# A gated delta rule scan: heads in halves, two products of the state beside each other, the decay on ScalarE, the last token tile finished by itself

## The reference, cut to what matters

```python
def step(state, inp):
    qd, wc, uc, kd, aqk, dl = inp
    v_new = uc - jnp.einsum('bhik,bhkv->bhiv', wc, state)
    o = jnp.einsum('bhik,bhkv->bhiv', qd, state) + jnp.einsum('bhij,bhjv->bhiv', aqk, v_new)
    state = state * dl[..., None, None] + jnp.einsum('bhik,bhiv->bhkv', kd, v_new)
    return state, o
...
state0 = jnp.zeros((bn, h, dk, dv), jnp.float32)
_, o = lax.scan(step, state0, xs)
...
y = (o * lax.rsqrt(jnp.mean(o * o, axis=-1, keepdims=True) + RMS_EPS)
     * norm_gain.astype(jnp.float32) * jax.nn.silu(zf))
```

## Time and profile before

| | us |
|---|---|
| median of three runs | 1775.05 |
| the profiled execution: its time | 1778.09 |
| the profiled execution: its span on the core | 1776.8 |

### The profile page before, as it was taken

How to read it: one execution, slowest core, us unless ns; L and a number is a source line. 1 busy time by engine, 2 the same in 40 slices (tenths; PEclk the granted TensorE clock), 3 DMA queues, 4 the chain that set the end, 5 groups by cost and what they waited for, 6 DMA issues and landing times.

```text
span 1776.8 us, 25041 instructions
## 1 busy us (share of the span) xinstructions
PE 1625.4 (91%) x9620; PEld 1177.3 (66%) x9620; DVE 922.4 (52%) x1873; ACT 694.2 (39%) x1518; POOL 347.1 (20%) x353
## 2 busy tenths in 40 slices
PE   6999869789999999989997799999999959999992
PEld 5887559667888888867877466667888733333330
DVE  4752665455766665664526866643435752223224
ACT  4432752353333334454322677764424421111111
POOL 0000643001222210000000455530010122333320
PEclk9999989899999999989998799999999969999997
DMA  6321000321444443323200000015223349999964
GB/s 273 115 95 48 1 2 3 143 95 58 188 181 190 189 178 154 131 95 141 97 0 25 1 8 8 8 36 232 95 93 145 142 166 383 394 370 392 385 249 159
DMA packets 40229, 251.74 MB, mean 142 GB/s; under 512 B 17904, under 2 KB 18032, under 8 KB 23600
## 3 DMA queue, kind: packets, MB, share of 16 engines
q1 hardware_dynamic: 23120, 223.49, 32.2%
q10 hardware_dynamic: 3168, 15.07, 2.2%
q0 software_dynamic: 13824, 11.58, 2.0%
HBM read 293.99 MB, written 18.87 MB: 176 GB/s over the span
## 4 chain that ended last, share of the span: by engine, by line
PE 85%; DVE 7%; DMA 3%; ACT 3%; issue 1%; SPq 0%; POOL 0%; DVEq 0%; ACTq 0%; POOLq 0%
PE banks L2222 17%; PE banks L2224 16%; PE banks L2223 16%; PE banks L2690 8%; PE banks L2160 7%; PE banks L2706 4%; PE banks L2283 3%; PE banks L2305 3%; DMA plain<-in_moe_gu,arena 2%; PE banks L2407 1%; PE banks L2569 1%; DVE units L1210 1%; ACT arena L629 1%; PE banks L2612 1%; PE banks L2539 0%
## 5 line engine op out<-in xcount | busy, mean ns | idle before, releaser
L629 ACT ACTIVATE units<-arena 128x512 fp32r<-128x512 f32 (+2 forms) x416 | 251.0, 626 | 482.1 <-PE banks L2224 477.3
L1210 DVE TENSOR_TENSOR units<-arena,units 128x512 fp32r<-128x512 f32 x370 | 252.2, 705 | 281.1 <-ACT units L629 280.8
L2222 PE MATMUL banks<-hx,units 128*128 128x512 f32 x800 | 316.3, 395 | 3.5 <-DVE arena L1663 1.7
L2224 PE MATMUL banks<-hx,units 128*128 128x512 f32 x800 | 313.3, 392 | 0.0
L2223 PE MATMUL banks<-hx,units 128*128 128x512 f32 x800 | 313.3, 392 | 0.0
L2222 PEld LDWEIGHTS banks<-hx,units 128*128 128x128 f32 x800 | 151.7, 190 | 35.5 <-issue 4.5
L2224 PEld LDWEIGHTS banks<-hx,units 128*128 128x128 f32 x800 | 151.4, 189 | 31.9
L2223 PEld LDWEIGHTS banks<-hx,units 128*128 128x128 f32 x800 | 151.7, 190 | 31.0
L2160 PE MATMUL banks<-arena 128*128 128x128 f32 (+2 forms) x752 | 118.1, 292 | 49.6 <-ACT arena L629 14.1
L629 ACT ACTIVATE arena<-banks 128x512 f32<-128x512 f32 (+3 forms) x194 | 106.7, 563 | 143.8 <-PE banks L2160 65.9
L2222 PE MATMUL banks<-units 128*128 128x512 f32 x380 | 150.8, 397 | 8.7 <-DVE units L1210 8.7
(11 more groups left out here) (420 smaller groups left out, 2448.6 us busy)
## 6 DMA issues: line engine op xcount, KB each, us to landing
arena<-in_moe_gu SPq DMA_DIRECT2D x32, 2048.0 KB, 10.0
arena<-in_w_in SPq DMA_DIRECT2D x17, 2048.0 KB, 8.6
arena<-in_moe_dn SPq DMA_DIRECT2D x32, 1024.0 KB, 9.8
arena<-in_ada SPq DMA_DIRECT2D x12, 2048.0 KB, 11.0
arena<-in_w_gu SPq DMA_DIRECT2D x11, 2048.0 KB, 8.5
arena<-in_w_out SPq DMA_DIRECT2D x4, 2048.0 KB, 8.5
arena<-in_w_down SPq DMA_DIRECT2D x4, 2048.0 KB, 10.6
arena<-in_cmp_w SPq DMA_DIRECT2D x2, 2048.0 KB, 8.5
```

The lines of the kernel that those rows point to most:

```text
L629: return func(dst, src, ACT.Copy, scale=scale)
L1210: tt(lo, src, hi.bitcast(F32), SUB).then_inc(*up("gemm_dve", "lo", c.part, u))
L2222: pe.matmul(bs[i], sh[:, q], mh, start=c.first and k == 0, stop=False)
L2224: return pe.matmul(bs[i], sl[:, q], mh, start=False, stop=c.last and k == c.kn - 1)
```

## The change

- TensorE gives `ws` and `dS` two banks each, one for each half of the heads (0 and 1, 2 and 3), and the waits on S and `vn` go by halves. VectorE's additions for `vn` and S go by halves as well, 256 columns each.
- `o` is written to the other 64 partitions (`other`), and head by head `ws` and the first `o` product are issued in turn.
- In chunk 0 the state is zero: `ws`, the first `o` product and the clearing of S are left out, `vn` is U itself, and the next state is a copy of `dS`.
- The decay `Sd` moves from VectorE to ScalarE, as four copies of 128x128 with a factor per partition.
- A small square root ahead of the scan brings in the function table; the means' roots are taken in two parts (`goA` for tiles 0 to 2, `goB` for tile 3).
- Tiles 0 to 2 are scaled and transposed first; tile 3 is scaled by VectorE in four instructions that include the gate z (GpSimd's fourth product goes), and its transposes go to two banks of their own (`yL`).
- The load of `gu0` now waits for that work of VectorE on tile 3.

```diff
@@ -940,19 +940,29 @@
     for t in range(4):
         a.wait_ge(*at("gdn_pe", "U", t))
         copy(m.U[:, t, :], s.bank("gdn", "U", t)).then_inc(*up("gdn_act", "U", t))
+    func(m.rs_tmp[:, 63:64], ones1, ACT.Sqrt)
     for c in range(8):
-        t, rows = c // 2, H64[c % 2]
+        t, rows, other = c // 2, H64[c % 2], H64[1 - c % 2]
+        if 0 < c < 7:
+            for h, q in enumerate(H4):
+                a.wait_ge(*at("gdn_dve", "S", c, h // 2))
+                copy(m.Sd[:, q], m.S[c % 2][:, q], m.dl[:, c, h:h + 1]).then_inc(*up("gdn_act", "Sd", c, h // 2))
+        if c == 7:
+            root("goA", g[:, 1, 0:12], m.rs_tmp[:, 0:12])
         a.wait_ge(*at("gdn_pe", "o", c))
-        copy(m.O[rows, t, :], s.bank("gdn", "o", c)[rows, :]).then_inc(*up("gdn_act", "O", c))
+        copy(m.O[rows, t, :], s.bank("gdn", "o", c)[other, :]).then_inc(*up("gdn_act", "O", c))
         if c % 2:
             a.wait_ge(*at("gdn_act", "O", c))
             for h in range(4):
                 func(m.osq[:, t, H4[h]], m.O[:, t, H4[h]], ACT.Square,
                      accum_out=g[:, 1, 4 * t + h:4 * t + h + 1]).then_inc(*up("gdn_act", "osq", t, h))
-    root("go", g[:, 1, :], m.rs_tmp[:, 0:16])
-    for f in (0, 2):
+    root("goB", g[:, 1, 12:16], m.rs_tmp[:, 0:4])
+    for f in range(4):
         a.wait_ge(*at("gdn_pe", "yT", f))
-        copy(m.yT[:, f, :], s.bank("gdn", "yT", f), C["gdn"][:, 0:1]).then_inc(*up("gdn_act", "yT", f))
+        copy(m.yT[:, f, 0:384], s.bank("gdn", "yT", f)[:, 0:384], C["gdn"][:, 0:1]).then_inc(*up("gdn_act", "yT", f))
+    a.wait_ge(*at("gdn_pe", "yL", 0))
+    copy(m.yT[:, 0:2, 384:512], s.bank("gdn", "yL", 0)[:, 0:256].rearrange("p (f k) -> p f k", f=2),
+         C["gdn"][:, 0:1]).then_inc(*up("gdn_act", "yL", 0))
     fence(9)
 
     a.dma_start(m.x, x_v).then_inc(*up("dma_x", by=16))
@@ -1598,31 +1608,43 @@
             v.wait_ge(*at("gdn_pe", "dXT", lv, t))
             tt(m.XT[:, t, :], m.XT[:, t, :], s.bank("gdn", "dXT", lv, t)[:, 0:256], SUB).then_inc(*up("gdn_dve", "XT", lv, t))
     v.wait_ge(*at("gdn_pe", "Y", 4, 3))
-    v.memset(m.S[0], 0.0).then_inc(*up("gdn_dve", "S", 0))
     for t in range(4):
         for c, rows in enumerate(H64):
             v.wait_ge(*at("gdn_pe", "W", t, c, 3))
             ts(hv(m.WT[:, t, :])[:, :, rows], hv(s.bank("gdn", "W", t, c)[:, 0:256]), -1.0, None,
                MUL).then_inc(*up("gdn_dve", "W", t, c))
+    two = [slice(0, 256), slice(256, 512)]
     for c in range(8):
         t, rows = c // 2, H64[c % 2]
-        S = m.S[c % 2]
-        v.wait_ge(*at("gdn_pe", "ws", c))
         v.wait_ge(*at("gdn_act", "U", t))
-        tt(m.vn[rows, :], s.bank("gdn", "ws", c)[rows, :], m.U[rows, t, :], ADD).then_inc(*up("gdn_dve", "vn", c))
-        if c < 7:
-            tt(hv(m.Sd), hv(S), bc(m.dl[:, c, :].unsqueeze(2), 4, 128), MUL).then_inc(*up("gdn_dve", "Sd", c))
-            v.wait_ge(*at("gdn_pe", "dS", c))
-            v.wait_ge(*at("gdn_dve", "Sd", c))
-            tt(m.S[1 - c % 2], m.Sd, s.bank("gdn", "dS", c), ADD).then_inc(*up("gdn_dve", "S", c + 1))
-    v.wait_ge(*at("gdn_act", "osq", 3, 3))
-    rstd("go", g[:, 1, :], g[:, 1, :], 128.0)
-    for t in range(4):
+        for half, q in enumerate(two):
+            if c:
+                v.wait_ge(*at("gdn_pe", "ws", c, half))
+                tt(m.vn[rows, q], s.bank("gdn", "ws", c, half)[rows, q], m.U[rows, t, q], ADD).then_inc(*up("gdn_dve", "vn", c, half))
+        for half, q in enumerate(two):
+            if c == 7:
+                break
+            v.wait_ge(*at("gdn_pe", "dS", c, half))
+            new, grown = m.S[1 - c % 2][:, q], s.bank("gdn", "dS", c, half)[:, q]
+            if c:
+                v.wait_ge(*at("gdn_act", "Sd", c, half))
+                ins = tt(new, m.Sd[:, q], grown, ADD)
+            else:
+                ins = v.tensor_copy(new, grown)
+            ins.then_inc(*up("gdn_dve", "S", c + 1, half))
+    v.wait_ge(*at("gdn_act", "osq", 2, 3))
+    rstd("goA", g[:, 1, 0:12], g[:, 1, 0:12], 128.0)
+    for t in range(3):
         v.wait_ge(*at("gdn_pool", "oz", t))
         tt(hv(m.O[:, t, :]), hv(m.O[:, t, :]), fac(1, t), MUL).then_inc(*up("gdn_dve", "on", t))
-    for f in (1, 3):
-        v.wait_ge(*at("gdn_pe", "yT", f))
-        ts(m.yT[:, f, :], s.bank("gdn", "yT", f), C["gdn"][:, 0:1], None, MUL).then_inc(*up("gdn_dve", "yT", f))
+    v.wait_ge(*at("gdn_act", "osq", 3, 3))
+    rstd("goB", g[:, 1, 12:16], g[:, 1, 12:16], 128.0)
+    for h, q in enumerate(H4):
+        ins = stt(m.O[:, 3, q], m.O[:, 3, q], g[:, 1, 12 + h:13 + h], m.z[:, 3, q], MUL, MUL)
+    ins.then_inc(*up("gdn_dve", "on", 3))
+    v.wait_ge(*at("gdn_pe", "yL", 1))
+    ts(m.yT[:, 2:4, 384:512], s.bank("gdn", "yL", 1)[:, 0:256].rearrange("p (f k) -> p f k", f=2),
+       C["gdn"][:, 0:1], None, MUL).then_inc(*up("gdn_dve", "yL", 1))
     fence(9)
 
     gemm("w_out0")
@@ -2498,34 +2520,43 @@
                           stop=True).then_inc(*up("gdn_pe", "W", t, c, h))
     for c in range(8):
         t, o = c // 2, 64 * (c % 2)
-        rows = slice(o, o + 64)
+        rows, other = H64[c % 2], H64[1 - c % 2]
         sc = [slice(128 * h + o, 128 * h + o + 64) for h in range(4)]
-        S = m.S[c % 2]
-        b = take(("gdn", "ws", c), ("gdn_dve", "vn", c))
+        S, vn = m.S[c % 2], m.vn if c else m.U[:, 0, :]
         pe.wait_ge(*at("gdn_dve", "W", t, c % 2))
-        pe.wait_ge(*at("gdn_dve", "S", c))
+        pe.wait_ge(*at("gdn_act", "U", t))
+        ob = take(("gdn", "o", c), ("gdn_act", "O", c))
+        if c:
+            wb = [take(("gdn", "ws", c, half), ("gdn_dve", "vn", c, half)) for half in range(2)]
+            for h, q in enumerate(H4):
+                if h % 2 == 0:
+                    pe.wait_ge(*at("gdn_dve", "S", c, h // 2))
+                pe.matmul(wb[h // 2][rows, q], m.WT[:, t, sc[h]], S[:, q], start=True, stop=True).then_inc(*up("gdn_pe", "ws", c, h // 2))
+                pe.matmul(ob[other, q], m.DT[:, t, sc[h]], S[:, q], start=h == 0, stop=False)
+        if c < 7:
+            db = [take(("gdn", "dS", c, half), ("gdn_dve", "S", c + 1, half)) for half in range(2)]
+            for h, q in enumerate(H4):
+                if c and h % 2 == 0:
+                    pe.wait_ge(*at("gdn_dve", "vn", c, h // 2))
+                pe.matmul(db[h // 2][:, q], m.Kd[rows, t, q], vn[rows, q], start=True, stop=True).then_inc(*up("gdn_pe", "dS", c, h // 2))
         for h, q in enumerate(H4):
-            ins = pe.matmul(b[rows, q], m.WT[:, t, sc[h]], S[:, q], start=True, stop=True)
-        ins.then_inc(*up("gdn_pe", "ws", c))
-        b = take(("gdn", "o", c), ("gdn_act", "O", c))
-        for h, q in enumerate(H4):
-            pe.matmul(b[rows, q], m.DT[:, t, sc[h]], S[:, q], start=h == 0, stop=False)
-        pe.wait_ge(*at("gdn_dve", "vn", c))
-        if c < 7:
-            b2 = take(("gdn", "dS", c), ("gdn_dve", "S", c + 1))
-            for q in H4:
-                ins = pe.matmul(b2[:, q], m.Kd[rows, t, q], m.vn[rows, q], start=True, stop=True)
-            ins.then_inc(*up("gdn_pe", "dS", c))
-        for h, q in enumerate(H4):
-            ins = pe.matmul(b[rows, q], m.PT[rows, t, Q4[h]], m.vn[rows, q], start=False, stop=h == 3)
+            if c == 7 and h % 2 == 0:
+                pe.wait_ge(*at("gdn_dve", "vn", c, h // 2))
+            ins = pe.matmul(ob[other, q], m.PT[rows, t, Q4[h]], vn[rows, q], start=c == h == 0, stop=h == 3)
         ins.then_inc(*up("gdn_pe", "o", c))
-    for f in range(4):
-        b = take(("gdn", "yT", f), (("gdn_act", "gdn_dve")[f % 2], "yT", f))
-        for t in range(4):
-            if f == 0:
-                pe.wait_ge(*at("gdn_dve", "on", t))
-            ins = tp(b[:, H4[t]], m.O[:, t, H4[f]])
-        ins.then_inc(*up("gdn_pe", "yT", f))
+    ybs = [take(("gdn", "yT", f), ("gdn_act", "yT", f)) for f in range(4)]
+    for t in range(3):
+        pe.wait_ge(*at("gdn_dve", "on", t))
+        for f in range(4):
+            ins = tp(ybs[f][:, H4[t]], m.O[:, t, H4[f]])
+            if t == 2:
+                ins.then_inc(*up("gdn_pe", "yT", f))
+    pe.wait_ge(*at("gdn_dve", "on", 3))
+    for half in range(2):
+        yl = take(("gdn", "yL", half), (("gdn_act", "gdn_dve")[half], "yL", half))
+        for f in range(2):
+            ins = tp(yl[:, H4[f]], m.O[:, 3, H4[2 * half + f]])
+        ins.then_inc(*up("gdn_pe", "yL", half))
     fence(9)
 
     gemm("w_out0")
@@ -2816,7 +2847,7 @@
         sp.dma_start(m.x0[:, t, :], x_v[:, t, :]).then_inc(*up(f"x_in{t}", by=16))
     for name in p.ring:
         if name == "gu0":
-            sp.wait_ge(*at("gdn_pool", "oz", 3))
+            sp.wait_ge(*at("gdn_dve", "on", 3))
         if name == "glu":
             for f in range(4):
                 place_T(f)
```

## The result

The changed kernel took 1760.24 us (median of five runs, 1758.99 to 1765.65) against 1775.23 for the kernel before on the same chip (five runs, 1774.62 to 1781.54): a ratio of the times of 0.9913, with a 95% interval of 0.989 to 0.9936, 15.0 us faster. Run again later beside other kernels it took 1757.34 (six runs, 1755.39 to 1760.24; before 1775.43), ratio 0.9894 [0.987, 0.9918]. The prediction was 1764.5, with a range of 1761.5 to 1768.5: the direction is right, the size is 4.3 us short.

A forecast was written before the change was run, and what follows sets the result against it. TensorE's four product groups in line bound the scan, a nearly equal chain beside them. Scan 7.2 plus tail 3.9 less clock 0.5 gave 10.6 saved: 1764.5 from 1775.05, range 1761.5 to 1768.5.

The forecast's parts named there:

- `dS` after the pair's start: Inside a scan chunk: half-wise `vn` lets `dS` start at 1.15, with a new TensorE pause of 0.13 before it.
- a chunk: Scan chunks 1 to 6: 3.25 us each in place of 4.01, 0.76 less, 4.56 in six.
- copy of `O` to the last copy of yT: Tail between scan and output projection: 7.05 in place of 10.98, 3.9 saved.
- clock behind the tail: First products of `w_out0`: low clock expected again, between 1.8 gained and 1.3 lost; 0.5 lost taken.
- everything behind: All work after the fence behind the tail: waits for it, so the 10.6 saved comes through whole.
- The scan's gain: Whole scan: 1.91 from chunk 0, 4.56 from chunks 1 to 6, 0.73 from chunk 7, together 7.2 saved.
- the ScalarE rival: Scan after odd chunks: decay queued behind ScalarE's squares makes S late, 1.1 lost in all, 1765.6; chance 0.09.
- Signals: Scan: 42 more signals from `ws` and `dS`, counted as nothing; by the skill's figure 1.1 us, forecast 1765.6.
- Loads in line: Rival, `ws` and `o` pair: weight loads queue, pair 1.50, chunk 3.60, 2.6 lost in all, 1767.1; chance 0.08.
- the six that were allowed for: Load of x beside `gu0` behind the tail: landing six later still leaves 7 in hand, so no cost.
- The clock: Rival in the scan: new pauses ahead of `dS` drop the clock, up to 13 slower, 1788; chance 0.03.
- the 0.05 for other effects: Chance left for a loss elsewhere that eats the gain, 0.04 of it within 0.2%.

The follow-up runs named there:

- both directions: Kernel before, bank turn set on by 7 behind the tail: 1770.5 (before 1776.23); changed kernel, turn set on by 1 there: 1765.03.
- that bank alone: Kernel before, with third and later transposed blocks at `gu0` first taking free banks the first two blocks don't use: 1771.5 (before 1775.43), ratio 0.9976.
- even groups: Changed kernel, with `ws` of all four heads issued first, then the first `o` of all four, still in the other columns: 1761.2, ratio 0.9924.

## Why the prediction was wrong

| step | predicted | measured |
|---|---|---|
| chunk 0 | 2.10 | 2.05 from `dS` (300.12) to the next pair; 4.00 before |
| pair of `ws` and `o` | 1.02 | 0.93 to 1.03 |
| `dS` after the pair's start | 1.15 | 1.33 |
| a chunk | 3.25 | 3.40 |
| chunk 7 to the copy of `O` | 2.28 | 2.37 |
| copy of `O` to the last copy of yT | 7.05 | 6.87 |
| clock behind the tail | 0.5 lost | 0 |
| up to `w_out0` | 10.6 | 10.3 |
| everything behind | comes through whole | 4.8 more at `gu0` |

**The step that failed** is "Everything behind waits for this fence, so it comes through whole." It looked at what waits for the fence in time, and not at what the program hands on: the turn of the banks. The sum up to `w_out0` was right within half a microsecond, in part by luck: from the first product of the scan to the copy of `O` it took 31.07 before and 24.86 after (6.2 saved, 7.2 predicted), the tail saved 4.1 (3.9 predicted), the clock lost nothing (0.5 predicted): 10.3. The scan's gain was put 1.0 too large, and the two others took 0.7 of that back. The changed kernel with its later banks as before took 1765.0, where 1764.5 was predicted. The missing part is the third block's bank, shown in both directions and by that bank alone. The profile of before showed the wait, 3.08 ahead of four transposes; a count of the banks taken, 27 against 42, would have shown that it moves.

**Chunks.** The mechanism was right, the size a quarter too large: 0.6 saved in each and not 0.76. The pair costs what the earlier trace rows gave. The error is the handover: the first half is issued by 0.49, as allowed (0.51), but seen at 0.76 and not at 0.66, so that 0.27 went by where the prediction had put 0.15, less than the 0.20 that it read from the earlier trace rows and with no row for the difference; and `dS` starts some 0.15 after `vn`'s half is done and not 0.07, so TensorE waits longer than the 0.13 that was allowed. The last `ws` of that half starts 0.38 after the pair and is seen 0.38 later; why so late stays open, but it is not the number of signals. All the saving comes from the columns, as argued from the earlier trace rows.

**Decay, S and ScalarE.** As predicted: no wait of TensorE for S, and less than 0.1 in hand after odd chunks, so the ScalarE rival fell by a margin as thin as it said. With the decay on VectorE, S of chunk 2 was complete at 309.29, 0.4 before the next pair (309.69), so that would have had more room.

**Signals.** Right to count nothing (they are 41 more and not 42: 56 in place of 15). The Trainium skill, "TensorE: Matmul & The Clock Gate", Part 3 (The cost: per-tile semaphore tail), would give an estimated 0.7 us for the 28 signals taken away; the chunk stayed at 3.41, so no run here shows that cost in a stream of products.

**Loads in line.** The rival fell: the loads of `ws` and `o` start together at 302.17. The Trainium skill, "TensorE: Matmul & The Clock Gate", Part 3 (The mechanism), lets a load overlap a running product only where row groups differ; both use all rows here, and different columns were enough. The measurement decides.

**Tail and SyncE.** Right within 0.2. The load of x took 5.8 longer beside `gu0`, near the six that were allowed for, and was hidden.

**The clock.** It neither fell in the scan nor cost more behind the tail (3.78 for nine products, 3.80 before). That term should have been 0. One reading ahead of it was off as well: in the kernel before, the granted clock was 1.00 from 332 to 334 and 0.57 from 334 to 336, so it fell some four microseconds behind the last product, which ends at 330.62, and not after five.

**Chances.** The forecast's own range began at 1761.6 and the 0.05 for other effects was all on the side of a loss. An effect elsewhere can have either sign.

## What to carry to other kernels

Where buffers are handed out in turn through a whole program, a change in how many one part takes renames every buffer behind it: count them modulo the pool, and look in the trace for waits whose releaser is merely the previous user of a buffer. Turning the pool alone, with no other change, separates that effect from the change itself, and should be run on both kernels before a difference far from the edit is explained. Where two products share a moving operand and each fills half the columns, put them in different halves: in the same half alternation gave nothing here (4.00 against 4.01), in different halves even groups gave 0.38 a chunk, and alternation 0.6.

## What the runs showed of the hardware that was not expected

The same twelve transposes in a row were not always followed by the same clock. From the first of them to the fourth block's it took 5.58 to 5.95 in twelve of fifteen profiles without the shared bank, and 7.03 to 7.15 in three, where the first seven products or so ran at a granted clock of 0.50 (1.2 GHz), 0.43 apart, before they came 0.23 apart (2.4 GHz); the two profiles with the shared bank took 10.36 and 10.66. The Trainium skill, "TensorE: Matmul & The Clock Gate", Part 1 (What's actually happening), says that the number of slow products at the start of one kernel varies from run to run; the traces agree for this later start, with one to four against seven or eight. What decides it here was not tried. So by these profiles removing the wait is worth 3.2 (10.36 against 7.15) to 5.1 (10.66 against 5.58) in one execution.

Behind `n1` the same happens between two executions of the changed kernel itself. Both have twelve transposes in a row and the same wait of 0.74, and then run at different clocks; the first window is of the first execution, the second of the later one:

```profile
776.12:780.00 3.88, 3.88 (x9) 3.11 (x10) 2.38 (x4) 0.11 (x1) 0.00 (x0) 0.50 0.00 0
776.55:780.40 3.85, 3.85 (x19) 3.22 (x20) 2.76 (x5) 0.93 (x3) 0.00 (x0) 1.00 0.00 0
```

From there to the end of TensorE's next long wait (804.42 and 802.13) it takes 28.30 in one and 25.58 in the other. These 2.7 us are most of the 3.0 by which the two spans differ, and no line of the kernel made them.
